# Hybrid decoder block: the first half of the output projection as products of 512 columns, and a register read moved on TensorE

## What is computed

```python
h = rmsnorm(x, attn_norm_g); proj = h @ w_mix_in          # 2,560 columns
y_conv = g_b * causal_short_conv(g_c * u, conv_w)          # 256 channels
y_diff = rmsnorm(diff_attention(q, k, v, lam, rel_bias))   # 4 heads, 512 wide
y_mem  = memory_attention(qm, rmsnorm(mem), w_mem_kv)      # 4 heads, 256 wide
x = x + concatenate([y_conv, y_diff, y_mem]) @ w_mix_out   # "mixing": 1,024 x 1,024 by 1,024 x 1,024
h = rmsnorm(x, ffn_norm_g)
logits = h @ router_w + router_b                           # top 4 of 32 experts, softmax over the 4
x = x + sum over the 4 chosen experts e of gate_e * (act(h @ w_gate_up[e] + b) @ w_down[e] + b_down[e])
out = rmsnorm(x, final_norm_g)
```

## Time and profile before

| | |
|---|---|
| median of 3 runs | 2203.84 us (2203.52 to 2205.39) |
| the profiled execution | 2204.53 us |
| its span, first to last instruction | 2202.9 us |
| mean granted TensorE clock | 0.98 |
| TensorE (PE) busy | 2115.6 us, 96% |
| weight loads of TensorE (PEld) busy | 1763.5 us, 80% |
| VectorE (DVE) busy | 1572.4 us, 71% |
| ScalarE (ACT) busy | 1335.9 us, 61% |
| GpSimd (POOL) busy | 363.9 us, 17% |

### The profile page before, as it was taken

How to read it: one execution, slowest core, us unless ns; L and a number is a source line. 1 busy time by engine, 2 the same in 40 slices (tenths; PEclk the granted TensorE clock), 3 DMA queues, 4 the chain that set the end, 5 groups by cost and what they waited for, 6 DMA issues and landing times.

```text
span 2202.9 us, 33789 instructions
## 1 busy us (share of the span) xinstructions
PE 2115.6 (96%) x10634; PEld 1763.5 (80%) x10635; DVE 1572.4 (71%) x1686; ACT 1335.9 (61%) x1531; POOL 363.9 (17%) x317
## 2 busy tenths in 40 slices
PE   7999999897899999999999999999999999999995
PEld 6889867897678888888888888888888888888884
DVE  4321189676677679789769999986776898677756
ACT  5111179444556567587657878775655777565745
POOL 1000000033412112122202112221111212111201
PEclk9999989998899999999999999999999999999998
DMA  5121300434798679799959999998777999767955
GB/s 204 58 77 57 115 1 1 172 116 130 181 372 299 215 237 375 258 361 380 348 198 363 373 378 372 379 365 269 241 233 234 343 378 365 239 226 247 330 179 190
DMA packets 267046, 543.01 MB, mean 246 GB/s; under 512 B 14725, under 2 KB 31391, under 8 KB 266896
## 3 DMA queue, kind: packets, MB, share of 16 engines
q1 hardware_dynamic: 248896, 490.48, 62.6%
q0 software_dynamic: 18096, 51.82, 9.6%
HBM read 501.78 MB, written 42.78 MB: 247 GB/s over the span
## 4 chain that ended last, share of the span: by engine, by line
PE 92%; DVE 4%; issue 2%; ACT 1%; DMA 1%; SPq 0%; POOL 0%; DVEq 0%; ACTq 0%; POOLq 0%
PE ps L765 87%; PE ps L1012 2%; PE ps L1005 2%; PE ps L897 1%; DMA weight_ring<-in_w_mix_in 0%; ACT hT_hi L1253 0%; DVE work L1536 0%; PE ps L952 0%; DVE weight_ring L1802 0%; DVE m_max L1497 0%; DVE work L1549 0%; DVE hT_lo L1451 0%; DVE slots_between L1726 0%; ACT weight_ring L1324 0%; DMA out_rows<-weight_ring 0%
## 5 line engine op out<-in xcount | busy, mean ns | idle before, releaser
L765 PE MATMUL ps<-hT_hi,hT_lo 128*128 128x512 f32 (+1 forms) x4256 | 1385.6, 390 | 1.0 <-DVE slots_between L1726 0.4
L765 PEld LDWEIGHTS ps<-hT_hi,hT_lo 128*128 128x128 f32 x4256 | 797.3, 188 | 167.7 <-issue 6.5
L1253 ACT ACTIVATE hT_hi<-weight_ring 128x2048 fp32r<-128x2048 f32 x417 | 785.6, 1912 | 181.8 <-PE ps L765 123.1
L1726 DVE TENSOR_TENSOR slots_between<-weight_ring,hT_hi 128x2048 fp32r<-128x2048 f32 x245 | 552.1, 2285 | 111.4 <-ACT hT_hi L1253 108.8
L765 PE MATMUL ps<-slots_between,hT_lo 128*128 128x512 f32 x1344 | 524.9, 391 | 0.0
L1726 DVE TENSOR_TENSOR w_lo<-weight_ring,hT_hi 128x2048 fp32r<-128x2048 f32 x140 | 319.9, 2285 | 34.9 <-ACT hT_hi L1253 34.9
L765 PE MATMUL ps<-w_lo,hT_lo 128*128 128x512 f32 (+1 forms) x896 | 335.5, 374 | 0.0
L765 PEld LDWEIGHTS ps<-slots_between,hT_lo 128*128 128x128 f32 x1344 | 253.3, 188 | 54.1
L765 PEld LDWEIGHTS ps<-w_lo,hT_lo 128*128 128x128 f32 x896 | 169.1, 189 | 27.3
L651 POOL DMA_INDIRECT residual_rows<-work,idx_now x47 | 116.4, 2476 | 373.8 <-ACT work L1314 252.7
L645 POOL DMA_INDIRECT work<-normed_rows,idx_far x49 | 70.6, 1441 | 528.8 <-PE ps L1005 415.0
(11 more groups left out here) (275 smaller groups left out, 2473.4 us busy)
## 6 DMA issues: line engine op xcount, KB each, us to landing
weight_ring<-in_w_gate_up SPq DMA_DIRECT2D x280, 1024.0 KB, 10.0
weight_ring<-in_w_down SPq DMA_DIRECT2D x140, 1024.0 KB, 9.3
weight_ring<-in_w_mix_in SPq DMA_DIRECT2D x10, 1024.0 KB, 9.7
weight_ring<-in_x SPq DMA_DIRECT2D x8, 512.0 KB, 8.1
weight_ring<-in_w_mix_out SPq DMA_DIRECT2D x4, 1024.0 KB, 7.1
work<-in_x SPq DMA_DIRECT2D x8, 512.0 KB, 6.3
residual_rows<-work SPq DMA_DIRECT2D x8, 512.0 KB
normed_rows<-work SPq DMA_DIRECT2D x8, 512.0 KB
```

Of the source, the lines that this page charges most:

```text
L765: return pe.matmul(o, l, r, start=first, stop=last)
L1253: act.activation(w_high_part(u), ring[:, home(u), :], ACT.Copy).then_inc(s["w_high_made"], 1)
L1726: dve.tensor_tensor(w_low_part(u), ring[:, home(u), :], w_high_part(u).bitcast(f32), ALU.subtract)\
```

## The change

Quarters 0 and 1 of a tile are made together. The new function `mix_first_half` makes 24 products of 512 columns where two calls of `mix_quarter` made 48 of 256. Its moving operand is read in two stretches of 256, one from each quarter's place. Output, sums and the order within the contraction stay as they were. Quarters 2 and 3 are unchanged. On its own, the read of the last item's number on TensorE moves ahead of the turns of the first item's rows.

```diff
+            def mix_first_half(i):
+                mhi, mlo = mix_parts(i)
+                whi = hT_hi[:, 0:4, :].rearrange("p k t -> p (k t)").rearrange("p (q k c) -> p k q c", q=2, k=KD)
+                wlo = w_lo_r[:, 0:2, :].rearrange("p q (k c) -> p k q c", k=KD)
+                to = ps[:, 2 * (i % 2), :]
+                for k in range(KD):
+                    mm(to, mhi[:, k, :], whi[:, k], k == 0, False)
+                    mm(to, mhi[:, k, :], wlo[:, k], False, False)
+                    last = mm(to, mlo[:, k, :], whi[:, k], False, k == KD - 1)
+                return last
+
@@
-                    mix_quarter(i, 0)
-                    mix_quarter(i, 1).then_inc(s["e_mix"], 1)
+                    mix_first_half(i).then_inc(s["e_mix"], 1)
@@
+            last = last_item(pe)
             for b in range(BLOCKS):
                 pe.wait_ge(s_gather[b], 16)
                 if b == 1:
@@
             pe.wait_ge(s["down_read"], NT)
             pe.sem_inc(s["w_used"], HI_SLOTS)
             pe.sem_inc(s["a_turned"], 1)
-            last = last_item(pe)
             with pe.Fori(0, MAX_ITEMS // GROUP) as group:
```

## The result

The change makes the kernel slower: 2224.57 us (median of 4 runs, 2222.2 to 2225.08) against 2204.26 us for the kernel before in the same measurement, a ratio of 1.009 with a 95% interval of 1.0078 to 1.0102. That is 20.3 us more. The forecast was 2200.7 us.

What follows compares the result with a forecast made beforehand. The prediction took TensorE's issue to bound the mixing stage and TensorE the items. Wider products 2.37, register load 0.8 and code place net 0 summed to 3.2 us, giving 2200.7 us; range 2195.9 to 2206.4.

Steps and rivals of the forecast that it cites:

- Net 0: TensorE's instruction blocks at two branches around the item loop: costs and savings cancel, from 5.8 us lost to 4.8 gained.
- rival D: Item loop outgrows TensorE's eight held blocks, redrawn in all 33 passages: 102 us lost, 2303 us; chance 0.18.
- the 3.1 us that line 401 was to give back: Line 401's long branch after item 0: one wait instead of two, about 3.1 us of its 6.18 saved.
- Wider products: Mixing stage's first halves on TensorE: 24 products of 512 columns replace 48 of 256 per tile, saving 2.37 us.
- rival B: Mixing stage: wider products run no faster because the second stretch starts anew; only the load gains, 2203.0 us; chance 0.12.
- The register load: TensorE's sequencer before the first item: the load moves into idle time ahead of the turns, saving 0.8 us.
- line 398's first jump: Branch on TensorE at the first item: should now miss one instruction block, costing about 2.8 us.
- rival C: First jump costs its block, second returns nothing because leapt-over blocks are drawn in turn; 2203.4 or 2206.4 us; chance 0.10.

Runs made afterwards that it cites:

- f1: The change with 126 never-run instructions behind a branch ahead of the item loop, shifting its start to the old place within a block; 2200.67 us, ratio 0.9984.
- e3: The wider products alone, added to the kernel before, with the register load left behind the turns; 2223.1 us, ratio 1.0086.
- e4: The kernel before with only the register load moved ahead of the turns; 2203.67 us, ratio 0.9997.
- g2: The change with tiles 0 and 1 left in products of 256 columns and tiles 2 to 7 wide; 2200.64 us, ratio 0.9984.

## Why the forecast was wrong

The step that failed is the term for where the code lies, "Net 0". It priced two branches, and put at nothing that the loop might need more blocks than TensorE holds; that was left to rival D, outside the range. The runs showed 20.2 us in the items in its place (12.7 of idle time, 7.5 of slow clock), and the 3.1 us that line 401 was to give back didn't come. Together they are 23.3 of the 23.9 us between the forecast, 2200.7, and the measured 2224.57.

**Wider products: right.** The step at 512 columns with the operand in two stretches is 227.6 ns, where 227.5 was taken from an item, so the second stretch costs nothing and rival B falls. The rule that the prediction took from the Trainium skill, TensorE: Matmul & The Clock Gate, section Back-to-back issue gap, would have made the fixed part worth 0.48 us in all; the page gives its 2.5 ns for an isolated product, and not for a stream such as this. The trace went the other way: in f1, and in e3 too, the way from the first head transpose of this stage to the last tile's transposes of normed rows takes 123.8 us instead of 125.9, a gain of 2.1 of the forecast's 2.37. The profiled execution of the change shows 1.1 of it. There the clock was low for 6.8 us at the stage's start instead of 3.4, and at that clock the wider product gains nothing.

**The register load: right.** With the loop in its old place the gain is the whole 0.8 us. It has to be read from the right mark. Behind the turns the sequencer waits for `bias_low`, that is, for VectorE's line 1865, and in all thirteen traces that wait ends 0.04 us behind this instruction, wherever the turns end (0.5 us ahead of it in f1, 1.2 behind it in the change). Line 1865 before, then line 1865 and the first product in e4:

```profile
561.47 2.28 DVE L1865 TENSOR_TENSOR mem_there<-region_bias,mem_there 32x2048 fp32r<-32x2048 f32 x1
```

```profile
562.04 2.28 DVE L1865 TENSOR_TENSOR mem_there<-region_bias,mem_there 32x2048 fp32r<-32x2048 f32 x1
...
568.01 0.79 PE L765 MATMUL ps<-mem_there,picked 128*128 128x512 f32 x1 [3.71 <-issue]
```

From its end to the first product it is 4.50 us before (563.75 to 568.25), 3.69 in e4 and 3.65 in f1. By its median e4, 0.6 us faster, can't be told from no change.

**Where the code lies, "Net 0": this step failed.** Of its two branches, the first came as forecast: line 398's first jump missed a block, and cost 3.0 us (from the end of VectorE's `bias_low` instruction to the first product it is 6.72 us in the change and 3.69 in e4; forecast 2.8). The second didn't. I read the 6.18 us of line 401 as two waits, of which the change would spare one. But that branch took 6.13 to 6.26 us in all eleven experiments, wherever it stood in its block (28.52 to 30.53), also with the next block long there. Behind the branch the queue is silent for 3.7 us and then draws once, in the kernel before (625.9, then 629.6) as in the change (626.4, then 630.1). So a far jump to a block that is absent has a price of its own, twice that of a near one, and no part of it was to be had back. So far the times are those of rival C; its reason, that the blocks leapt over are drawn in turn, isn't shown, since the packets carry no block numbers.

**Rival D had the mechanism and the wrong price.** It named the ninth block, the place and the packets that would show it, and got 0.18 and a time of 2303 us. The error is in its count, "in every passage": 33 passages, with idle time ahead of every item, where the ring loses its blocks only when a ninth is used in between, which three items do. Had I walked the kinds of the items through a ring of eight, D would have stood at three stalls of 3 to 6 us and the clock behind them, 9 to 24 us, and the range would have had to reach there. The price of one stall is 4.4 us of idle time (13.2 for three), though its branch takes 5.4 to 5.6 us: the matmuls already handed on cover the rest. Another 7.5 us went to the clock. I had seen the clock at 0.57 behind the gap of the earlier trace rows and priced it at 1.7 us, but only for the one gap, and not for the gaps that D would add.

The Trainium skill, Runtime: NRT & Kernel Launch, section Instruction fetch mechanics, gives TensorE's instruction memory as 128 KiB in blocks of 16 KiB, which is the eight that the packets show. The same section says that a taken branch out of a window of two pages stalls. The trace disagrees for this engine: in the kernel before, every passage jumps back over up to six blocks and nothing is drawn after 636 us.

**The version to keep** is g2: 2200.64 us, 0.16% below the kernel before and 1.1% below the change, with no instruction that is of no use. It gives up two tiles' gain, by the forecast's terms 0.3 us for tile 1 and 0.2 for tile 0. f1, all eight tiles wide and shifted, gains 4.05 us on the kernel before of its round and g2 3.41 on that of its own; the 0.6 us between them go the right way but lie within both intervals. In the profiled executions the stage's gain is 2.1 us in f1 and 1.7 in g2.

## What to carry to other kernels

A loop on TensorE that leaps among bodies is cheap as long as its code, with the block that is drawn ahead, touches no more than eight blocks of 256 instructions between two uses of any of them, and its end stays clear of the next edge (by this count of instructions 67 were enough, and 43 not); past that it cost 0.8 to 5.8% in these runs. So taking instructions out ahead of such a loop is not free: count where it begins and ends, look at the packets of the instruction queue behind the loop's first passages (none is right), and shift it with code that is leapt over, or with a choice like that of g2. Before pricing an eviction, walk the real sequence of bodies through the ring, and add the slow products behind each stall.

## What was not expected of the hardware

- 64 semaphore increments in a row on TensorE took some 10 us, 0.15 us each, though the records of such instructions show 51 ns. Here they were no free padding, even in idle time.
- The first jump far ahead (line 401 behind item 0), to a block not yet drawn, took 6.13 to 6.26 us in all thirteen traces. A near one (the first of line 398, where it was late) took 3.36 to 3.67 us. The way back to the loop's head, once the ring had turned over, took 5.1 to 5.7 us in the change and in the kernels with its three stalls.
- The clock made 37% of the items' loss (7.5 of 20.2 us): behind idle time of 4 to 5 us TensorE ran at 1.2 GHz for 3.4 or 6.8 us, and which of the two it was differed between stalls of the same length.
